# Streaming encoder step: the feed-forward norm's weights applied to the tokens before they are split into parts, and the out-projection's last steps placed behind each of its blocks

## What is computed

```python
x = x + (g_sb * (o_sb @ w_sb_o) + g_sw * (o_swa @ w_swa_o)) @ w_out      # out-projection
h = rms_norm(x, g_ffn)                                                  # x * rsqrt(mean(x*x) + eps) * g_ffn
logits = h @ [w_rg, w_re] + bias        # 4 groups, 16 experts: best group, best two experts in it
y = sum over the two of  gate * ((silu(h @ w_gate[e]) * (h @ w_up[e])) @ w_down[e])
out = rms_norm(x + y, g_final)
```

## Time and profile before

| | us |
|---|---|
| median of three runs (1405.9 to 1408.04) | 1407.13 |
| the profiled execution | 1406.63 |
| its span | 1404.9 |
| first expert matmul, from the span's start | 820.9 |

### The profile page before, as it was taken

The page is one execution under the profiler, slowest core; times in us unless marked ns, Lnnn a source line. Parts: engine busy times, 40 slices in busy tenths (PEclk is TensorE's granted clock), DMA queues, the critical chain, the costliest instruction groups (busy, mean ns, idle before and its releaser), DMA issues.

```text
span 1404.9 us, 21804 instructions
## 1 busy us (share of the span) xinstructions
PE 1237.1 (88%) x8932; PEld 1075.3 (77%) x8932; DVE 936.7 (67%) x894; ACT 786.3 (56%) x746; POOL 61.7 (4%) x105
## 2 busy tenths in 40 slices
PE   5889999979999899999999776999889999999870
PEld 3789999969889899999999555666666666666550
DVE  3633445643544554454444785999999999999977
ACT  3423332235665554545323654888888887888852
POOL 2100010011221000000000000000000000000000
PEclk9899999979999999999999878999999999999995
DMA  8474544531332345435648446999999999999924
GB/s 259 166 285 158 176 163 169 180 130 60 119 119 96 128 136 179 169 130 179 215 152 305 173 155 217 388 392 398 401 407 399 402 406 402 400 405 398 411 86 192
DMA packets 186431, 340.93 MB, mean 243 GB/s; under 512 B 5248, under 2 KB 107760, under 8 KB 175488
## 3 DMA queue, kind: packets, MB, share of 16 engines
q1 hardware_dynamic: 182208, 320.36, 61.9%
q0 software_dynamic: 3760, 16.17, 3.4%
q10 hardware_dynamic: 400, 3.51, 0.6%
HBM read 319.51 MB, written 20.71 MB: 242 GB/s over the span
## 4 chain that ended last, share of the span: by engine, by line
PE 49%; DVE 33%; ACT 8%; issue 6%; DMA 3%; DVEq 0%; ACTq 0%; POOL 0%; POOLq 0%; SPq 0%
DVE slot_lo L353 21%; PE bank L923 14%; PE bank L925 13%; PE bank L924 13%; PE bank L1135 3%; ACT eh L358 2%; DVE y_sb L1595 2%; ACT wh L613 2%; DMA ring<-in_w_in 1%; DVE hg L1568 1%; DVE hgx L1574 1%; PE bank L1145 1%; PE bank L901 1%; DVE wl L1285 1%; DMA con<-in_const 1%
## 5 line engine op out<-in xcount | busy, mean ns | idle before, releaser
L353 DVE TENSOR_TENSOR slot_lo<-slot,eh 128x2048 fp32r<-128x2048 f32 x192 | 432.5, 2281 | 9.3 <-ACT eh L358 9.2
L358 ACT ACTIVATE eh<-slot 128x2048 fp32r<-128x2048 f32 x192 | 361.7, 1909 | 49.6 <-PE bank L1138 28.7
L1285 DVE TENSOR_TENSOR wl<-ring,wh 128x2048 fp32r<-128x2048 f32 x100 | 229.1, 2293 | 217.6 <-ACT wh L613 217.5
L923 PE MATMUL bank<-xh,wh 128*128 128x288 f32 x1088 | 332.2, 305 | 9.7 <-DVE xl L1293 5.8
L924 PE MATMUL bank<-xl,wh 128*128 128x288 f32 x1088 | 324.8, 299 | 0.0
L925 PE MATMUL bank<-xh,wl 128*128 128x288 f32 x1088 | 323.9, 298 | 0.0
L613 ACT ACTIVATE wh<-ring 128x2048 fp32r<-128x2048 f32 x100 | 190.8, 1909 | 144.8 <-PE bank L925 133.5
L923 PEld LDWEIGHTS bank<-xh,wh 128*128 128x128 f32 x1088 | 207.5, 191 | 14.6 <-issue 7.7
L924 PEld LDWEIGHTS bank<-xl,wh 128*128 128x128 f32 x1088 | 208.4, 192 | 0.3
L925 PEld LDWEIGHTS bank<-xh,wl 128*128 128x128 f32 x1088 | 208.5, 192 | 0.0
L1135 PE MATMUL bank<-slot_lo,hgx 128*128 128x512 f32 x512 | 146.1, 408 | 24.6 <-DVE slot_lo L353 22.7
(11 more groups left out here) (313 smaller groups left out, 1529.5 us busy)
## 6 DMA issues: line engine op xcount, KB each, us to landing
ring<-in_w_in SPq DMA_DIRECT2D x34, 2048.0 KB, 7.9
slot<-in_w_e_gate SPq DMA_DIRECT2D x64, 1024.0 KB, 9.4
slot<-in_w_e_up SPq DMA_DIRECT2D x64, 1024.0 KB, 9.8
slot<-in_w_e_down SPq DMA_DIRECT2D x64, 1024.0 KB, 10.4
ring<-in_w_out SPq DMA_DIRECT2D x8, 2048.0 KB, 7.9
ring<-in_w_sb_o SPq DMA_DIRECT2D x8, 1024.0 KB, 5.2
ring<-in_w_swa_o SPq DMA_DIRECT2D x8, 1024.0 KB, 7.5
y_rows<-y_sb SPq DMA_DIRECT2D x15, 512.0 KB, 10.0
```

Of the source, the lines that this page charges most:

```text
L353: v.tensor_tensor(slot_lo[i][:], slot[i][:], eh[t % EH][:].bitcast(F32), ALU.subtract)\
L358: a_.activation(eh[t % EH][:], slot[t % CH][:], ACT.Copy).then_inc(S["hi_ready"], 1)
L923: mm_(dst, wh[:, j % 2, k, :], hi[:, k, :], start=(k == k0), stop=False)
L1285: v.tensor_tensor(wl[:, j % 2], raw(j), wh[:, j % 2].bitcast(F32), ALU.subtract)\
```

## The change

The norm's weights `g_ffn` are multiplied into `xT`'s blocks on ScalarE ahead of the transposes (`xg`), so that the parts `x2` hold weighted tokens; `gathered` and `hg` go, and the experts' tokens are split straight from PSUM. The out-projection is written out for all 16 blocks. Behind block k TensorE turns block k-1 and adds its logits; ScalarE squares block k and weights it; VectorE adds the squares up, and TensorE sums them over the features at the end (`ssq`). The rows are split in five groups (of 4, 4, 4, 2 and 2 blocks); the last group's remainders and low parts come behind `masks` and the first `choose`. Expert 0's tokens are split in two halves. Since `x2` no longer holds plain `x`, POOL writes `xT` out to `x2_spill`, SP loads it again as `xb` near the end, and `x2_back` becomes transposes of it. Places of `yb` and `gfin` move. The path for experts with more than 64 tokens is changed likewise.

```diff
+X2G = ((0, 4), (4, 4), (8, 4), (12, 2), (14, 2))
+LAST = {k0 + n - 1: g for g, (k0, n) in enumerate(X2G)}
+AFTER = {4: 0, 8: 1, 12: 2, 14: 3}
+    xg = at("xg", 201, [P, 2, NT])
+    xb = at("xb", 72, [P, KT, NT])
     hgx = at("hgx", 162, [P, KT, 2 * SLOTS], F32R)
-    hg = at("hg", 170, [P, KT, SLOTS])
...
+            def final_loads():
+
+                sp.wait_ge(S["x2_out"], 16 * 4)
+                sp.dma_start(xb[:], x2_spill.rearrange("p (k n) -> p k n", k=KT)).then_inc(S["x2_in"], 16)
+                sp.wait_ge(S["used"], NE * CH - CH + 5)
...
+            for i in range(4):
+                pool.wait_ge(S["ev_d"], EV_OUT_D + 2 + 4 * i + 3)
+                pool.dma_start(x2_spill[:, 4 * i * NT:(4 * i + 4) * NT].rearrange("p (k n) -> p k n", k=4),
+                               xT[:, 4 * i:4 * i + 4, :]).then_inc(S["x2_out"], 16)
...
-            with act.Fori(0, IT_END - IT_OUT - 1) as i:
-                for j in range(4):
...
+            def parts_high(g):
+
                 for t, n in enumerate(TILES):
-                    act.wait_ge(S["x2_ps"], 3 * q + t + 1)
-                    a_.activation(x2_part(0, t, q), x2_bank(q, t)[0:n], ACT.Copy)
+                    act.wait_ge(S["x2_ps"], 3 * g + t + 1)
+                    a_.activation(x2_part(0, t, g), x2_bank(g, t)[0:n], ACT.Copy).then_inc(S["x2_a"], 1)
                 for t, n in enumerate(TILES):
-                    act.wait_ge(S["x2_r"], 3 * q + t + 1)
-                    a_.activation(x2_part(1, t, q), x2r[t][0:n], ACT.Copy).then_inc(S["x2_b"], 1)
+                    act.wait_ge(S["x2_r"], 3 * g + t + 1)
+                    a_.activation(x2_part(1, t, g), x2r[t][0:n, 0:X2G[g][1] * P], ACT.Copy).then_inc(S["x2_b"], 1)
+
+            for k in range(KT):
+                it, j = IT_OUT + k // 4, k % 4
+                if k < KT - 2:
+                    step(it, j, None, slot1 + 16 * (k // 4 + 1))
+                act.wait_ge(S["ev_d"], EV_OUT_D + 2 + k)
+                if k >= 2:
+                    act.wait_ge(S["sq_sum"], k - 1)
+                    if k - 2 in LAST:
+                        act.wait_ge(S["x2_ps"], 3 * LAST[k - 2] + 3)
+                    else:
+                        act.wait_ge(S["xg_turned"], sum(i not in LAST for i in range(k - 1)))
+                a_.activation(sq[k % 2], xT[:, k, :], ACT.Square).then_inc(S["sq_done"], 1)
+                a_.activation(xg[:, k % 2, :], xT[:, k, :], ACT.Identity, scale=par[:, 48 + k:49 + k])\
+                    .then_inc(S["xg_done"], 1)
+                if k in AFTER:
+                    parts_high(AFTER[k])
             act.wait_ge(S["rms"], 3)
             a_.activation(stat[:, 16:19], stat[:, 4:7], ACT.Sqrt).then_inc(S["rms"], 1)
+            parts_high(4)
...
-                act.wait_ge(S["hg_sb"], s + 1)
-                if s:
+                if s == 0:
+                    act.wait_ge(S["hg_half"], 1)
+                    a_.activation(hgx[:, 0:8, 0:SLOTS], hg_ps(0, 8), ACT.Copy).then_inc(S["hgh_half"], 1)
+                else:
                     act.wait_ge(S["used"], WHEN[s - 1, 7] + 1)
-                a_.activation(hgx[:, :, 0:SLOTS], hg[:], ACT.Copy).then_inc(S["hgh_done"], 1)
+                act.wait_ge(S["hg_ps"], s + 1)
+                k0 = 0 if s else 8
+                a_.activation(hgx[:, k0:, 0:SLOTS], hg_ps(k0, KT), ACT.Copy).then_inc(S["hgh_done"], 1)
...
             act.wait_ge(S["blk"], upto(IT_END - 1, 3))
+            act.wait_ge(S["x2_out"], 16 * 4)
             for t in range(EH):
...
-            with pe.Fori(0, IT_END - IT_OUT - 1) as i:
-                for j in range(4):
-                    pe.wait_ge(S["ev_d"], i * 4 + (EV_OUT_D + j))
-                    products(i + IT_OUT, j, mh, ml)
...
-            for j in range(4):
-                pe.wait_ge(S["ev_d"], EV_OUT_D + 12 + j)
-                products(IT_END - 1, j, mh, ml)
-                if j:
-                    token_major(j - 1)
-                if j == 1:
+            def turn_x(k):
+
+                g = next(g for g, (k0, n) in enumerate(X2G) if k0 <= k < k0 + n)
+                k0, nk = X2G[g]
+                pe.wait_ge(S["xg_done"], k + 1)
+                for t, n in enumerate(TILES):
+                    if k == k0 and 3 * g + t >= 4:
+                        pe.wait_ge(S["x2_r"], 3 * g + t - 3)
+                    mm = tr(x2_bank(g, t)[0:n, (k - k0) * P:(k - k0 + 1) * P], xg[:, k % 2, tok(t)], ident)
+                    if k == k0 + nk - 1:
+                        mm.then_inc(S["x2_ps"], 1)
+                if k < k0 + nk - 1:
+                    mm.then_inc(S["xg_turned"], 1)
+
+            def logits(k):
+
+                return mm_(ps[7][0:NL, 0:NT], wr[:, k, :], xT[:, k, :], start=(k == 0), stop=(k == KT - 1))
+
+            def ssq(src, first):
+
+                for t, n in enumerate(TILES):
+                    mm = mm_(ssq_bank(t), src[:, tok(t)], ones[:, 0:1], start=first, stop=not first)
+                return mm
+
+            for k in range(KT):
+                pe.wait_ge(S["ev_d"], EV_OUT_D + k)
+                products(IT_OUT + k // 4, k % 4, mh, ml)
+                if k:
+                    turn_x(k - 1)
                     pe.wait_ge(S["wr_scaled"], 1)
-                if j > 1:
-                    logits(6 * j - 12, 6 * j - 6)
+                    logits(k - 1)
+            pe.wait_ge(S["ev_d"], EV_OUT_D + KT)
+            pe.wait_ge(S["sq_sum"], KT - 1)
+            pe.wait_ge(S["x2_r"], 3 * 4)
+            ssq(sqacc, True)
             pe.wait_ge(S["ev_d"], EV_OUT_D + KT + 1)
-            logits(12, KT)
-            token_major(3)
+            logits(KT - 1).then_inc(S["lg_ps"], 1)
+            pe.wait_ge(S["sq_done"], KT)
+            ssq(sq[(KT - 1) % 2], False).then_inc(S["ssq_ps"], 1)
+            turn_x(KT - 1)
             pe.wait_ge(S["lgT_done"], 1)
...
             pe.wait_ge(S["picked"], 1)
             for k in range(KT):
+                if k == X2G[4][0]:
+                    pe.wait_ge(S["x2_d"], 3 * 5)
                 mm = gather(k, pick[0])
+                if k == 7:
+                    mm.then_inc(S["hg_half"], 1)
-                if j == 0:
+                if t == 0:
+                    pe.wait_ge(S["hgl_half"], 1)
+                if j == (0 if e else 2):
                     pe.wait_ge(S["hgl_done"], e + 1)
...
-                if j < 7 and e + 1 < NE:
-                    if j == 0:
+                if (2 if e == 0 else 0) <= j < 7 and e + 1 < NE:
+                    if j == (0 if e else 2):
                         pe.wait_ge(S["picked"], e + 2)
-                        pe.wait_ge(S["hg_sb"], e + 1)
-                    k0 = (0, 2, 4, 7, 10, 12, 14, 16)
+                    k0 = (0, 2, 4, 7, 10, 12, 14, 16) if e else (0, 0, 0, 4, 7, 10, 13, 16)
                     for k in range(k0[j], k0[j + 1]):
                         mm = gather(k, pick[(e + 1) % 2])
...
+                for k in range(KT):
+                    mm = tr(ps[4 * (1 - t % 2) + k // 4][0:n, k % 4 * P:(k % 4 + 1) * P], xb[:, k, tok(t)], ident)
                 mm.then_inc(S["x2_back"], 1)
...
-            with dve.Fori(0, IT_END - IT_OUT - 1) as i:
-                for j in range(4):
-                    residual(i + IT_OUT, j, flat(xT[:, ds(i * 4 + j, 1), :]))
-                    split((j + 2) % 4, i * 4 + (4 * IT_OUT + j + 3))
...
+
+                w = X2G[g][1] * P
                 for t, n in enumerate(TILES):
-                    dve.wait_ge(S["x2_a"], 3 * q + t + 1)
-                    if q:
-                        dve.wait_ge(S["x2_d"], 3 * q + t - 2)
-                    v.tensor_tensor(x2r[t][0:n], x2_bank(q, t)[0:n], x2_part(0, t, q), ALU.subtract)\
+                    dve.wait_ge(S["x2_a"], 3 * g + t + 1)
+                    if g:
+                        dve.wait_ge(S["x2_d"], 3 * g + t - 2)
+                    v.tensor_tensor(x2r[t][0:n, 0:w], x2_bank(g, t)[0:n], x2_part(0, t, g), ALU.subtract)\
                         .then_inc(S["x2_r"], 1)
+
+            def parts_low(g):
+
+                w = X2G[g][1] * P
+                dve.wait_ge(S["x2_r"], 3 * g + 3)
+                own(v.tensor_copy(x2m[:, 0:w], x2r[2][0:DEC, 0:w]))
-                    dve.wait_ge(S["x2_b"], 3 * q + t + 1)
-                    v.tensor_tensor(x2_part(2, t, q), x2r[t][0:n], x2m[:] if t == 2 else x2_part(1, t, q),
+                    v.tensor_tensor(x2_part(2, t, g), x2r[t][0:n, 0:w], x2m[:, 0:w] if t == 2 else x2_part(1, t, g),
                                     ALU.subtract).then_inc(S["x2_d"], 1)
 
-            for j in range(4):
-                residual(IT_END - 1, j, xT[:, KT - 4 + j, :])
-                if j < 2:
-                    split(j + 2, upto(IT_END - 1, j + 2))
+            def add_squares(k):
+
+                dve.wait_ge(S["sq_done"], k + 1)
+                if k == 0:
+                    v.tensor_copy(sqacc, sq[0]).then_inc(S["sq_sum"], 1)
+                else:
+                    dve.wait_ge(S["sq_sum"], k)
```

(79 more changed lines are left out.)

60 lines of the change are left out of this document (16 added, 44 removed).

## The result

| kernel | device time, median (range) | ratio to before, 95% interval |
|---|---|---|
| before | 1407.59 us (1405.9 to 1409.12, 4 runs) | |
| changed | 1389.72 us (1389.64 to 1391.26, 4 runs) | 0.9881 [0.9866, 0.9896] |

What follows compares the result with a forecast made beforehand. VectorE was taken to set the experts' pace (32.70 us each), with DMA a little slower behind a store of loaded slots. Gain 6.9 + 13.2 - 0.5 = 19.6 us; 1406.6 - 19.6 = 1387.0, range 1382 to 1396.

Steps and rivals of the forecast that it cites:

- Step 1, blocks of the out-projection: Out-projection: transposes and a logit behind each block cost 0.83 us a block, so the last product ends 6.0 us later.
- Step 2, from the last product to the masks: Between the out-projection's last product and the masks: 9.7 us in place of 20.0, masks 4.3 us earlier.
- Step 3, to the first matmul: From masks to first expert matmul: 9.95 us in place of 11.7; VectorE's next split at +10.5, 5.3 us earlier.
- Step 4, handover: Handover to expert 1: its removed multiply gives 1.6 of 2.2 us, so the steady run starts 6.9 us earlier.
- Step 4, steady run: Experts' steady run: 14 removed multiplies save 1.14 us each, VectorE's period becomes 31.56 us, VectorE alone gains 16.0.
- Step 5, DMA: Experts' loads: the store of loaded slots runs dry in the last two or three experts; 13.2 of 16.0 us count.
- one of the prediction's own signs of being wrong: Last expert load: part 3 is wrong if its landing is not about 7 us earlier.
- the rival in which DMA keeps up: Experts' loads: the 0.3 us surplus an expert may come from bunched issues, VectorE decides to the end; 1384.2, chance 0.23.
- Behind the last slot: End of the kernel: nothing gets shorter; `xb` on SP's queue ahead of the last `y_rows` costs 0.5 us.

Runs made afterwards that it cites:

- no_mul: The kernel before with only the multiply by the norm's weights left out of the experts' tokens (expert 0 to 15): 1390.45 us.
- mul_back: The changed kernel with the multiply of the gathered tokens put back on VectorE for experts 1 to 15, its product unused: 1407.02 us.
- logit_pairs: The changed kernel with the logits of two blocks issued together behind every second block of the out-projection: 1389.96 us (one run).
- no_mul_gather: The kernel before without the multiply of the experts' tokens, and with expert 1's gathers placed as in the changed kernel: 1391.87 us.
- thin_two: The changed kernel without the second half of every expert slot's low part, with a second buffer for the experts' output rows: 1368.49 us (one run).
- no_mul_late: The kernel before without the multiply of the experts' tokens, and with VectorE's row steps moved behind the tenth slot: 1383.66 us.

## Why the prediction came out as it did

1389.7 lies 2.7 over the forecast of 1387.0 and inside its range. But that nearness is luck, a sum of errors of both signs: -4.5 ahead of the steady run, +2.9 in it, -1.0 behind it.

*Step 1, blocks of the out-projection: the mechanism held, the price was low.* TensorE has no stall (20.00 of 20 us at clock 1.00). But a block grew by 7.51 - 6.40 = 1.11 us, not 0.83: 0.42 for three transposes where the row of twelve gave 0.33, 0.59 for the logit where the row of six gave 0.50, and 0.10 more for the first matmul of the next product. 14 x 1.11 = 15.5 in place of 11.6; less the 5.7 that went, the last product should end 9.8 us later, not 6.0. In the profiled run it ended 8.1 later (797.3), as its first block was 1.5 us shorter than that of before (6.47 and 8.00). That is no work of the change: the granted clock from 680 to 685 was 1.00 behind a wait of 2.70 us, and 0.66 before, behind 3.08. In the old order it was 1.00 too (no_mul, behind 3.08), and in the new one 0.68 and 0.50 (mul_back and logit_pairs, behind 2.71). So some 1.6 of the 2.4 us by which the masks come earlier are luck.

*Step 2, from the last product to the masks*: 9.7 forecast, 9.4 measured, in place of 20.0. Steps 1 and 2 together are worth 20.0 - 9.4 - 9.8 = 0.8 us, in place of 4.3. no_mul's handover is 1.8 us shorter than the changed kernel's, so there is nothing left by which the new order could be faster.

*Step 3, to the first matmul*: +9.95 forecast, +10.0 measured; VectorE's next split +10.5, measured +10.4. The exponentials stand where they were put, and the run with them ahead shows that they cost. The Trainium skill, page "ScalarE: Activation LUTs", section "What ACT_TABLE_LOAD costs", would have had 1.38 us of drain on top; the load took 1.28 us (808.41) and the first exponential started at 809.71, 0.02 behind it: the trace does not bear that out here:

```profile
808.41 1.28 ACT L811 ACT_TABLE_LOAD   x1
809.71 0.21 ACT L811 ACTIVATE rt<-rt 128x12 f32<-128x12 f32 x1
```

*Step 4, handover: wrong, in sign.* It gave 1.6 us to the removed multiply of expert 1 and the splits behind it. From VectorE's next split to slot 12 it took 870.93 - 820.74 = 50.2 us before and 868.49 - 817.13 = 51.4 after: 2.8 us off, 1.2 longer and not 1.6 shorter. The step looked at the wait for L1568 and not at what ends last in that stretch: VectorE's row steps, TensorE's wait for the split behind them, and TensorE at a lower clock after it. The multiply there is worth 1.3 (63.1 - 61.8, mul_back); the gathers' new places take back about 0.6 (no_mul_gather), and the lead of the next split ends in a longer wait of TensorE (2.44 us at 834.45 before, 6.11 at 830.83 after). no_mul has that in the old order: from the next split to slot 12 it takes 50.3 us, no less than before, though the multiply is gone. How the remaining 1.9 us split up is open.

*Step 4, steady run: right.* 14 x 1.14 = 16.0 by VectorE's pace; the period is 31.56 as forecast, and the multiply put back takes the whole of it away.

*Step 5, DMA: the mis-sized term.* It put DMA's pace at 33.0 us an expert, from a time to landing that grew from 7.7 to 10.7 us over ten experts. The pace is 31.9 (thin_two), so against 31.56 the store loses no more than some 0.3 an expert, and it ends at 12.2 us instead of running dry; all 16.0 count, not 13.2. The last landing came 17.5 us earlier (1321.4 and 1338.9), not about 7, so one of the prediction's own signs of being wrong came true. The growth says nothing of DMA's pace: in the changed kernel, with 1.14 us less an expert, the same load's time grew as fast (8.6 us at 997.34, 11.4 nine experts later at 1281.47). Nor was it steady: in the kernel before, this load (KB, us to landing) issued at 1168.06 and at 1233.46 takes

```profile
slot<-in_w_e_up SPq DMA_DIRECT2D x1, 1024.0 KB, 10.8
...
slot<-in_w_e_up SPq DMA_DIRECT2D x1, 1024.0 KB, 9.6
```

before the 10.7 of the earlier trace rows, and in mul_back, at the same pace, 10.1 (1069.88) and 10.0 (1298.82). So the rival in which DMA keeps up was right about this term, though not for its reason: DMA is full at 413, and VectorE is just as full. The Trainium skill, page "DMA: Bandwidth & Descriptors", section "Where 436 GB/s comes from", gives 435 GB/s at the ports; these loads came to 414 to 415. The same section has about 358 bind for loads from HBM; one core alone did better here all along.

*Behind the last slot* 54.2 us passed in place of 52.7, where 0.5 was forecast for `xb`. It is not shown to be the change's: the runs without the multiply have the old end, and took 1388.7 - 1334.53 = 54.2 and 1381.5 - 1328.80 = 52.7 from ScalarE's last copy (no_mul, no_mul_late):

```profile
1334.53 1.90 ACT L362 ACTIVATE eh<-slot 128x2048 fp32r<-128x2048 f32 x1
```

```profile
1328.80 1.90 ACT L362 ACTIVATE eh<-slot 128x2048 fp32r<-128x2048 f32 x1
```

The wait for the gathered rows varies by that much from execution to execution (chain of waits: start, us; before, after, no_mul, no_mul_late):

```profile
1370.48 10.44 DMA yb<-y_rows,rows
1351.93 12.00 DMA yb<-y_rows,rows
1352.92 11.78 DMA yb<-y_rows,rows
1347.13 10.39 DMA yb<-y_rows,rows
```

## What to carry to other kernels

Time gained ahead of a stage counts only up to the wait that ends last in that stage: before pricing a lead, follow TensorE and VectorE through the stretch where it would be spent, as 7.1 us of steps needed only at the end were worth 7 to 9 us there. A growing time to landing is no measure of DMA's pace; take the consumers' work away and see at what rate the slots come. And price a small matmul by the block it is put into, not by its mean in a row of its own kind.

## What the runs showed of the hardware

A logit of two fp32 matmuls costs TensorE 0.50 us in a row of six, 0.54 in a pair (1.08 from 746.40 to 747.48), and 0.59 alone between transposes and products, with 0.10 more on the product behind them. One core moved 414 to 415 GB/s, nearly all of it loads from HBM, at a DMA share of 1.04 whether VectorE was busy 60 or 99 of 100 us; the same share stood at 1.03 when only 401 were moved, so the share does not show the last 3%.
